# Gate and up of eight experts as three-part products with the high and low weights under 320 and 160 columns, their weights in 512 KB pieces over eleven half slots

## The chip, the cores and the metric

The kernel runs on 1 core of one Trainium2 chip. The metric is the device time of one execution in microseconds: 2761.57 us, the median of 3 runs.

## The reference, cut to what matters

A model of four layers over 512 tokens of width 1024: attention parts, feed-forward parts, a short convolution, and one layer of eight experts. The change touches the layer of experts. For each token two of eight experts are chosen, and each expert computes

```
h = silu(xb @ w_gate[e]) * (xb @ w_up[e])      # 1024 -> 1408
out = (h @ w_down[e]) * w                      # 1408 -> 1024
```

on the rows that chose it; the results are added to the tokens. Everything is float32. The weights of one expert are 3 x 1024 x 1408 numbers, 17.3 MB.

## The kernel before, in words

The program is one stream per engine, with semaphores between them and no scheduler: the order of each engine's work is the order of its Python loops. P is 128 and NE 8; KD = 8 tiles of 128 make the width of 1024, KE = 11 tiles of 128 make an expert's hidden width of 1408. Each expert has room for CAP = 160 rows: a main part of 128 and a tail of 32 (TAIL).

**Loads.** SP issues the weights in the order of a queue, `chunks`, which PE's code fills with `take_slot` (line 617): five ring slots of 1 MB, and each load first waits for the semaphore of the slot's last use. A gate and up chunk is one tile of 128 columns of each, so its rows in memory are 512 bytes long. Down chunks hold two tiles of 128 rows, 4 KB long each.

**Three-part products.** Most products of the kernel work on float32r numbers, in which a float32 is a high part, rounded by a copy, and a low part, the difference. `matmul3` issues high x high, high x low and low x high. In the other parts of the model POOL makes both parts of the weights (lines 2193 and 2195). In the experts' gate and up this was not done: `up_pairs` (line 989) calls `fmajor` (line 832), whose matmul at line 836 multiplies raw float32 weights by raw float32 tokens, 160 columns. The trace shows each such product as two weight loads and two matmuls.

**One expert.** PE runs 11 pairs of a gate and an up tile (line 836), then `down` (line 1234): the tails of six tiles at full precision (line 1252, four at a time beside each other, 32 weight columns each), the transposes that gather the next expert's rows (`gather`, line 1192), three-part products of the main rows (lines 1268 to 1270) for six tiles, the other five tails, and the last five tiles. ACT applies SiLU (line 1856), rounds h (line 1922) and the down weights (line 1917, three high buffers), copies the gathered tokens with their gain (line 1902), and stores the results (lines 1971 to 1981). DVE multiplies gate and up (line 2789) and makes the low parts of h (line 2982) and of the down weights (line 2994, in place of the raw ones).

**Beside it.** POOL prepares matrices for the S5 part of a later layer, from SBUF to SBUF, with one semaphore after most instructions (lines 2312 to 2475). Four times PE turns such matrices (`turn_s5`, line 1299), twice it multiplies them (`intra_runs`, line 1311), once it turns the last expert's slots. Before, these run beside the fourth tile of experts 1 to 5. In the last expert POOL fetches the other experts' results by row (line 2491) and DVE adds them, weighted, to the tokens (`add_results`, line 2966): eight additions of 1024 columns. `scatter_last` (line 1228) then puts the last expert's rows back by a product.

## Time and profile before

| | |
|---|---|
| Median of 3 runs | 2761.57 us (2757.92 to 2771.27) |
| Profiled execution, own time | 2766.07 us |
| Its span | 2764.3 us |
| PE busy | 2668.6 us (97%), 13787 matmuls |
| DVE busy | 1164.6 us (42%) |
| ACT busy | 766.2 us (28%) |
| POOL busy | 1609.5 us (58%) |
| Mean DMA rate over the span | 134 GB/s |

The times of single instructions come from the profiled execution. Matmuls are pipelined: the duration of one holds its way through the array, so the pace of a stream is read from the distance between starts, or from a count over a window. PEld is the weight load, which runs beside the matmul before it. The DMA share is the mean busy share of 16 DMA engines and can exceed 1 where packets wait in them.

### The profile page before, as it was taken

What the parts mean: (1) busy time and instruction counts of PE and PEld (TensorE: products, weight loads), DVE (VectorE), ACT (ScalarE), POOL (GpSimd) and SP (SyncE); (2) the same over time, 40 slices, a digit from 0 to 9 for tenths busy, and PEclk for the clock granted to TensorE, in tenths of its full rate; (3) what the DMA queues carried; (4) which work ended last, traced back from release to release, by engine and by line L of the source; (5) the groups of instructions that cost most, each with busy time, mean ns of one, the idle gap of its engine ahead of it and who ended that gap; (6) DMA issues with size and microseconds to landing.
All of it is one profiled execution on the core that took longest, in us unless ns stands there. A gap on an engine that the chain in (4) does not pass through costs nothing.

```text
span 2764.3 us, 36674 instructions
## 1 busy us (share of the span) xinstructions
PE 2668.6 (97%) x13787; PEld 2142.2 (77%) x13787; DVE 1164.6 (42%) x2147; ACT 766.2 (28%) x1812; POOL 1609.5 (58%) x1778
## 2 busy tenths in 40 slices
PE   7999899999999899999999899899999998999999
PEld 3536578888888799999989576788888876788887
DVE  1156623213256323222243626557165347365372
ACT  2256621001110223232322414522022226421120
POOL 2235477777777431524362353578788662688785
PEclk9999999999999999999999999999999999999999
DMA  6741033233433399989899522433332312533331
GB/s 190 177 107 31 1 89 95 84 107 103 140 117 91 109 265 280 276 267 299 251 282 286 190 62 76 119 92 99 99 100 69 100 46 102 139 92 95 100 100 42
DMA packets 449183, 371.06 MB, mean 134 GB/s; under 512 B 16926, under 2 KB 388327, under 8 KB 448362
## 3 DMA queue, kind: packets, MB, share of 16 engines
q1 hardware_dynamic: 429504, 321.62, 39.4%
q0 software_dynamic: 12240, 33.00, 4.0%
q10 hardware_dynamic: 7258, 14.03, 2.1%
q8 instruction: 113, 1.85, 0.3%
q14 instruction: 68, 0.56, 0.1%
HBM read 335.59 MB, written 32.41 MB: 133 GB/s over the span
## 4 chain that ended last, share of the span: by engine, by line
PE 90%; DVE 4%; issue 2%; ACT 2%; DMA 1%; POOL 1%; ACTq 0%; DVEq 0%; SPq 0%; POOLq 0%
PE bank L654 19%; PE bank L656 19%; PE bank L655 19%; PE bank L836 15%; PE bank L848 2%; PE bank L1268 1%; PE bank L1252 1%; PE bank L931 1%; PE bank L1269 1%; PE bank L1270 1%; PE bank L900 1%; PE bank L948 1%; PE bank L957 1%; PE bank L914 1%; PE bank L717 1%
## 5 line engine op out<-in xcount | busy, mean ns | idle before, releaser
L2195 POOL TENSOR_TENSOR unit_parts<-ring,unit_parts 128x512 fp32r<-128x512 f32 x580 | 807.8, 1393 | 48.4
L2193 POOL TENSOR_SCALAR unit_parts<-ring 128x512 fp32r<-128x512 f32 x580 | 427.3, 737 | 359.6 <-PE bank L656 323.5
L654 PE MATMUL bank<-x_hi,unit_parts 128*128 128x512 f32 x1408 | 553.2, 393 | 0.8 <-issue 0.8
L656 PE MATMUL bank<-x_hi,unit_parts 128*128 128x512 f32 x1408 | 548.4, 389 | 0.0
L655 PE MATMUL bank<-x_lo,unit_parts 128*128 128x512 f32 x1408 | 548.0, 389 | 0.0
L836 PE MATMUL bank<-arena,ring 128*128 128x160 f32 x2816 | 384.8, 299 | 0.8 <-ACT arena L1902 0.8
L836 PEld LDWEIGHTS bank<-arena,ring 128*128 128x128 f32 x2816 | 383.4, 190 | 1.8 <-ACT arena L1902 1.0
L654 PE MATMUL bank<-unit_parts,hid_parts 128*128 128x512 f32 x784 | 307.9, 393 | 2.4 <-DVE hid_parts L2724 1.8
L654 PEld LDWEIGHTS bank<-x_hi,unit_parts 128*128 128x128 f32 x1408 | 264.5, 188 | 57.8 <-issue 2.8
L656 PEld LDWEIGHTS bank<-x_hi,unit_parts 128*128 128x128 f32 x1408 | 264.3, 188 | 55.6
L655 PEld LDWEIGHTS bank<-x_lo,unit_parts 128*128 128x128 f32 x1408 | 264.5, 188 | 54.3 <-issue 1.0
L655 PE MATMUL bank<-unit_parts,hid_parts 128*128 128x512 f32 x784 | 305.2, 389 | 0.0
L656 PE MATMUL bank<-unit_parts,hid_parts 128*128 128x512 f32 x776 | 302.3, 390 | 0.0
L2154 ACT ACTIVATE arena<-arena,vec 128x512 f32<-128x512 f32 x88 | 71.9, 817 | 464.4 <-DVE arena L3222 464.4
L2735 DVE TENSOR_TENSOR x<-bank,x 128x512 f32<-128x512 f32 x80 | 55.2, 691 | 331.7 <-PE bank L656 331.7
L2789 DVE TENSOR_TENSOR arena<-bank,arena 128x160 f32<-128x160 f32 x88 | 28.6, 324 | 359.7 <-PE bank L836 352.2
L654 PEld LDWEIGHTS bank<-unit_parts,hid_parts 128*128 128x128 f32 x784 | 147.2, 188 | 33.6 <-issue 3.9
L655 PEld LDWEIGHTS bank<-unit_parts,hid_parts 128*128 128x128 f32 x784 | 147.3, 188 | 30.4 <-issue 0.5
L656 PEld LDWEIGHTS bank<-unit_parts,hid_parts 128*128 128x128 f32 x776 | 145.7, 188 | 30.7
L2994 DVE TENSOR_TENSOR ring_lo<-ring,down_hi 128x1024 fp32r<-128x1024 f32 x88 | 111.5, 1300 | 51.5 <-ACT down_hi L1917 31.7
L3226 DVE SCALAR_TENSOR_TENSOR arena<-arena,vec 128x511 f32<-128x511 f32 x88 | 79.0, 898 | 77.9 <-ACT arena L2154 77.9
L1917 ACT ACTIVATE down_hi<-ring 128x1024 fp32r<-128x1024 f32 x88 | 92.7, 1060 | 66.9 <-PE bank L1270 52.5
(398 smaller groups left out, 3602.6 us busy)
## 6 DMA issues: line engine op xcount, KB each, us to landing
ring<-in_moe_w_gate SPq DMA_DIRECT2D x88, 512.0 KB, 6.6
ring<-in_moe_w_up SPq DMA_DIRECT2D x88, 512.0 KB, 7.4
ring<-in_w_up SPq DMA_DIRECT2D x88, 512.0 KB, 5.1
ring<-in_moe_w_down SPq DMA_DIRECT2D x40, 1024.0 KB, 5.7
ring<-in_w_down SPq DMA_DIRECT2D x16, 1024.0 KB, 5.0
ring<-in_od_w_in SPq DMA_DIRECT2D x24, 512.0 KB, 4.5
ring<-in_ffn_w_gate SPq DMA_DIRECT2D x22, 512.0 KB, 4.0
ring<-in_ffn_w_up SPq DMA_DIRECT2D x22, 512.0 KB, 5.3
```

Source lines behind the costliest of these rows:

```text
L654: pe.matmul(ps, a[0], b[0], start=start, stop=False)
L655: pe.matmul(ps, a[0], b[1], start=False, stop=False)
L656: return pe.matmul(ps, a[1], b[0], start=False, stop=stop)
L836: ins = pe.matmul(ps[rows_at:rows_at + m, 0:n], w[:, k * width + at:k * width + at + m], src[:, k, :], start=k == 0, stop=k == KD - 1)
L848: ins = pe.matmul(ps[:, :], weights(k), xnT[:, k, :], start=k == 0, stop=k == KD - 1)
L1917: act.activation(down_hi[:, n % DOWN_HI, :], raw, ACT.Copy).then_inc(S("down_rounded"), 1)
L2154: act.activation(acc[:, 2 * a + n % 2, :], unscaled[:, a, :], ACT.Identity, scale=vcol("conv_w_2", 132 * l + 88 + f), bias=vcol("conv_b_2" ...
L2193: pool.tensor_scalar(hi, raw, 1.0, 1.0, ALU.mult, ALU.mult).then_inc(S("units_rounded"), 1)
L2195: pool.tensor_tensor(lo, raw, hi.bitcast(F32), ALU.subtract).then_inc(S("units_split"), 1)
L2735: drain(dve.tensor_tensor(xs, ps[:, :], xs, ALU.add), key)
L2994: dve.tensor_tensor(lo, raw, down_hi[:, n % DOWN_HI, :].bitcast(F32), ALU.subtract)\
L3226: link(dve.scalar_tensor_tensor(out=o[:, 1:T], in0=b[:, 0:T - 1], scalar=vcol("conv_w_2", 132 * l + 44 + f), in1=o[:, 1:T], op0=ALU.mult, ...
```

## The change

Gate and up become three-part products. The gathered tokens are kept as a high and a low part side by side, 320 columns (`xe`). For each weight tile PE issues two products into one PSUM bank: the high weights under all 320 columns, the low weights under the first 160. Columns 0 to 159 then hold high x high + low x high, and 160 to 319 hold high weights x low tokens. ACT copies the second half out (`copy_low`), DVE adds the first to it (`sum_parts`) and drains the bank. SiLU, the product of gate and up and both parts of h now work on blocks of two tiles (`BLOCKS` = 6, the last with one tile), in SBUF.

Weights come in 33 pieces of 512 KB per expert: 22 of gate and up, 11 of down. A gate or up piece is four tiles of rows by two tiles of columns, with rows of 1 KB, but for the last block's (eight by one, 512 bytes). ACT rounds every piece, four ahead of PE's, into one of six high buffers (three lie over the normed tokens, `xnT`); DVE makes every low part, three ahead, in place of the raw piece. The ring's slots are used as ten halves, and an eleventh half lies over `xnT`. So `xnT` is first saved to DRAM by a 2 MB transfer on ACT's queue (`xn_saved`); a rare branch for overfull experts loads it again. The first piece lands in that half, after the save.

The tails of the down weights are placed two tiles at a time from piece 18 on (`TAILS_AFTER`), the gathering of the next expert's rows after piece 25. The turns of S5 matrices move to the blocks in `TURNS_AT`, into PSUM banks that the next block uses. In the last expert the additions of results stand after DVE's last split. The first expert's tokens wait for both parts before PE starts. The tail of the last expert's results is split after its main rows instead of before. The core of the diff (declarations, the branch for overfull experts and what is removed are left out; the removed functions are told above):

```diff
+BLOCKS = (KE + 1) // 2
+UP_PIECES = 4 * (KE // 2) + 2
+PIECES = UP_PIECES + KE
+TAILS_AFTER = {UP_PIECES - 4 + k: tuple(range(k, min(k + 2, KE))) for k in range(0, KE, 2)}
+GATHER_AT = UP_PIECES + 3
+HALVES = 11
 DOWN_HI = 3
+HI_BUFS = DOWN_HI + 3
+ROUND_AHEAD, SPLIT_AHEAD = 4, 3
+TURNS_AT = {(1, 1): ("turn", 0), (1, 4): ("turn", 1), (2, 2): ("intra", 0), (3, 1): ("turn", 2),
+            (3, 4): ("turn", 3), (4, 2): ("intra", 1), (5, 1): ("slots", 0)}
+OVER_BANKS = 4
...
+        xn_dram = nc.dram_tensor("normed_turned", (P, KD * T), F32).ap()
...
+            half_at, slot_users = [0], {}
+            xn_kept = [None, (), (S("xn_saved"), 16), None]
+            def take_half(part):
+                i = half_at[0]
+                half_at[0] = (i + 1) % HALVES
+                if not pieces:
+                    slot_users.update(users[0])
+                slot, second = divmod(i - own_halves, 2)
+                earlier = users[0].get(SLOTS + i) or (slot_users.get(slot) if slot >= 0 else xn_kept)
+                entry = [SLOTS + i, (part,), None, earlier]
+                users[0][SLOTS + i] = entry
+                if slot >= 0:
+                    users[0][slot] = entry
+                chunks.append(entry)
+                of, at = (landed, slot) if slot >= 0 and second else (landed_half, i)
+                of[at] += 16
+                return i, (half_landed[i], of[at]), entry
...
+            def turned_by(e, at):
+                return (at + e) % BANKS
+            def piece_source(e, p):
+                if p >= UP_PIECES:
+                    k = p - UP_PIECES
+                    return 1, D, A["moe_w_down"][0, e][k * P:(k + 1) * P, :]
+                b, up = p // 4, p % 2
+                W = A["moe_w_up" if up else "moe_w_gate"][0, e]
+                if b == BLOCKS - 1:
+                    return KD, P, W[:, 2 * b * P:(2 * b + 1) * P]
+                k0 = 4 * (p % 4 // 2)
+                return 4, 2 * P, W[k0 * P:(k0 + 4) * P, 2 * b * P:(2 * b + 2) * P]
+            def take_pieces(last):
+                for n in range(len(pieces), last + 1):
+                    kn, w, src = piece_source(*divmod(n, PIECES))
+                    i, arrived, entry = take_half((0, kn, w, src))
+                    pieces.append(dict(raw=half_raw[i], lo=half_lo[i], hi=piece_hi[n % HI_BUFS], arrived=arrived,
+                                       used=None, entry=entry))
+            def used_by(n, done):
+                pieces[n]["used"] = pieces[n]["entry"][2] = done
+            def rows_used(ins):
+                used[0] += 1
+                ins.then_inc(S("rows_used"), 1)
+                return S("rows_used"), used[0]
+            def up_piece(n):
+                e, p = divmod(n, PIECES)
+                b, up = p // 4, p % 2
+                take_pieces(n)
+                kn, w, _ = piece_source(e, p)
+                jn, k0 = w // P, 0 if kn == KD else 4 * (p % 4 // 2)
+                last = k0 + kn == KD
+                if k0 == 0:
+                    for j in range(jn):
+                        claim(("up", f"moe{e}", 2 * b + j, up), at=turned_by(e, 4 * (b % 2) + jn * up + j))
+                piece = pieces[n]
+                pe.wait_ge(S("piece_split"), n + 1)
+                for j in range(jn):
+                    key = ("up", f"moe{e}", 2 * b + j, up)
+                    ps = bank(key)
+                    for k in range(k0, k0 + kn):
+                        cols = slice((k - k0) * w + j * P, (k - k0) * w + (j + 1) * P)
+                        if k == KD - 1:
+                            pe.matmul(ps[:, 0:CAP], piece["lo"][:, cols], xe[:, k, 0:CAP], start=False, stop=False)
+                            ins = pe.matmul(ps[:, 0:2 * CAP], piece["hi"][:, cols], xe[:, k, :], start=False, stop=True)
+                        else:
+                            pe.matmul(ps[:, 0:2 * CAP], piece["hi"][:, cols], xe[:, k, :], start=k == 0, stop=False)
+                            ins = pe.matmul(ps[:, 0:CAP], piece["lo"][:, cols], xe[:, k, 0:CAP], start=False, stop=False)
+                    if last:
+                        fill(ins, key)
+                used_by(n, filled_sem(key) if last else rows_used(ins))
...
+            def down_rows(n):
+                e, p = divmod(n, PIECES)
+                k = p - UP_PIECES
+                if k == 0:
+                    for m in range(2):
+                        claim(("y", e, m), at=turned_by(e, 7 + m))
+                piece = pieces[n]
+                pe.wait_ge(S("piece_split"), n + 1)
+                pe.wait_ge(S("hidE_split"), BLOCKS * e + k // 2 + 1)
+                for m in range(2):
+                    cols = slice(m * 512, (m + 1) * 512)
+                    ins = matmul3(bank(("y", e, m))[:, :], (hidE_hi[:, k, :], hidE_lo[:, k, :]),
+                                  (piece["hi"][:, cols], piece["lo"][:, cols]), k == 0, k == KE - 1)
                     if k == KE - 1:
+                        fill(ins, ("y", e, m))
+                used_by(n, filled_sem(("y", e, 1)) if k == KE - 1 else rows_used(ins))
+            def down_tail(n):
+                e, p = divmod(n, PIECES)
+                k = p - UP_PIECES
+                take_pieces(n)
+                if k == 0:
+                    claim(("y", e, 2), at=turned_by(e, 6))
+                tail, piece = bank(("y", e, 2)), pieces[n]
+                pe.wait_ge(*piece["arrived"])
+                pe.wait_ge(S("hid_made"), KF + BLOCKS * e + k // 2 + 1)
+                for q in range(4):
+                    ins = pe.matmul(tail[32 * q:32 * q + 32, 0:256], hidE[:, k, P:CAP],
+                                    piece["raw"][:, 256 * q:256 * q + 256], start=k == 0, stop=k == KE - 1)
+                if k == KE - 1:
+                    fill(ins, ("y", e, 2))
+                else:
+                    ins.then_inc(S("raw_read"), 1)
...
+            for n in range(NE * PIECES):
+                e, p = divmod(n, PIECES)
+                if p == 0:
+                    for k0 in range(0, KD, PER_BANK):
+                        wait_drained(pe, ("xg", e, k0))
+                if p < UP_PIECES:
+                    up_piece(n)
+                    if p % 4 == 2 and (e, p // 4) in TURNS_AT:
+                        turn_runs(e, p // 4)
+                else:
+                    down_rows(n)
+                for k in TAILS_AFTER.get(p, ()):
+                    down_tail(PIECES * e + UP_PIECES + k)
+                if p == GATHER_AT and e + 1 < NE:
+                    gather(e + 1)
...
+            for half in range(2):
+                wait_drained(act, ("nt", "od_ffn", NT - 1, half))
+            act.dma_start(xn_dram.rearrange("p (k t) -> p k t", k=KD), xnT[:, :, :]).then_inc(S("xn_saved"), 16)
...
+            def round_piece(n):
+                act.wait_ge(*pieces[n]["arrived"])
+                if n >= HI_BUFS:
+                    act.wait_ge(*pieces[n - HI_BUFS]["used"])
+                act.activation(pieces[n]["hi"], pieces[n]["raw"], ACT.Copy).then_inc(S("piece_rounded"), 1)
+            def copy_low(e, b, up):
+                n = BLOCKS * e + b
+                if n >= 2:
+                    act.wait_ge(S("hid_made"), KF + n - 1)
+                for j in tiles_of(b):
+                    ps = wait_filled(act, ("up", f"moe{e}", j, up))
+                    act.activation((ups if up else gates)[n % 2][:, j % 2, :], ps[:, CAP:2 * CAP], ACT.Copy)\
+                       .then_inc(S("lows_copied"), 1)
+            def gate(e, b):
+                n = BLOCKS * e + b
+                wait_drained(act, ("up", f"moe{e}", tiles_of(b)[-1], 0))
+                g = gates[n % 2][:, 0:len(tiles_of(b)), :]
+                act.activation(g, g, ACT.Silu).then_inc(S("silu_done"), 1)
+            def round_hid(e, b):
+                n = BLOCKS * e + b
+                act.wait_ge(S("hid_made"), KF + n + 1)
+                cols = slice(tiles_of(b)[0], tiles_of(b)[-1] + 1)
+                act.activation(hidE_hi[:, cols, :], hidE[:, cols, 0:P], ACT.Copy).then_inc(S("hidE_rounded"), 1)
...
+            for n in range(DOWN_HI):
+                round_piece(n)
+            act.wait_ge(S("xn_saved"), 16)
+            for n in range(DOWN_HI, ROUND_AHEAD):
+                round_piece(n)
             gather(0)
+            for n in range(NE * PIECES):
+                e, p = divmod(n, PIECES)
+                if n + ROUND_AHEAD < NE * PIECES:
+                    round_piece(n + ROUND_AHEAD)
+                if e and p == 2:
+                    store_y(e - 1)
+                if p % 4 == 0 and (e, p // 4 - 1) in TURNS_AT:
+                    turn_runs(e, p // 4 - 1)
+                for b in range(BLOCKS):
+                    gate_at, up_at = (4 * b + 2, 4 * b + 3) if b < BLOCKS - 1 else (UP_PIECES - 2, UP_PIECES - 1)
+                    if p == gate_at + 2:
+                        copy_low(e, b, 0)
+                    if p == up_at + 2:
+                        copy_low(e, b, 1)
+                    if p == up_at + 4:
+                        gate(e, b)
+                    if p == up_at + 6:
+                        round_hid(e, b)
+                if e == 0 and p == 20:
+                    load_first_rows()
+                if p == GATHER_AT + 2 and e + 1 < NE:
                     gather(e + 1)
+            store_y(NE - 1)
...
+            def split_piece(n):
+                e, p = divmod(n, PIECES)
+                dve.wait_ge(S("piece_rounded"), n + 1)
+                if p == PIECES - 1:
+                    wait_filled(dve, ("y", e, 2))
+                elif p >= UP_PIECES:
+                    dve.wait_ge(S("raw_read"), (KE - 1) * e + p - UP_PIECES + 1)
+                dve.tensor_tensor(pieces[n]["lo"], pieces[n]["raw"], pieces[n]["hi"].bitcast(F32), ALU.subtract)\
+                   .then_inc(S("piece_split"), 1)
+            def split_tokens(e):
+                for k0 in range(0, KD, PER_BANK):
+                    ps = wait_filled(dve, ("xg", e, k0))
+                    rows_n[0] += 1
+                    dve.wait_ge(S("rows_rounded"), rows_n[0])
+                    for k in range(k0, min(KD, k0 + PER_BANK)):
+                        ins = dve.scalar_tensor_tensor(out=xe[:, k, CAP:2 * CAP], in0=ps[:, (k - k0) * CAP:(k - k0 + 1) * CAP],
+                                                       scalar=vcol("od_ffn_norm", k), in1=xe[:, k, 0:CAP].bitcast(F32),
+                                                       op0=ALU.mult, op1=ALU.subtract)
+                    drain(ins, ("xg", e, k0))
...
+            def sum_parts(e, b, up):
+                to = (ups if up else gates)[(BLOCKS * e + b) % 2]
+                for j in tiles_of(b):
+                    key = ("up", f"moe{e}", j, up)
+                    lows_n[0] += 1
+                    dve.wait_ge(S("lows_copied"), lows_n[0])
+                    drain(dve.tensor_tensor(to[:, j % 2, :], bank(key)[:, 0:CAP], to[:, j % 2, :], ALU.add), key)
+            lows_n = [0]
+            def multiply(e, b):
+                n = BLOCKS * e + b
+                jn = len(tiles_of(b))
+                wait_drained(dve, ("up", f"moe{e}", tiles_of(b)[-1], 1))
+                dve.wait_ge(S("silu_done"), KF + n + 1)
+                dve.tensor_tensor(hidE[:, 2 * b:2 * b + jn, :], ups[n % 2][:, 0:jn, :], gates[n % 2][:, 0:jn, :], ALU.mult)\
+                   .then_inc(S("hid_made"), 1)
+            def split_hid(e, b):
+                n = BLOCKS * e + b
+                cols = slice(tiles_of(b)[0], tiles_of(b)[-1] + 1)
+                dve.wait_ge(S("hidE_rounded"), n + 1)
+                dve.tensor_tensor(hidE_lo[:, cols, :], hidE[:, cols, 0:P], hidE_hi[:, cols, :].bitcast(F32), ALU.subtract)\
                    .then_inc(S("hidE_split"), 1)
+            for n in range(SPLIT_AHEAD):
+                split_piece(n)
+            split_tokens(0)
+            for n in range(NE * PIECES):
+                e, p = divmod(n, PIECES)
+                if n + SPLIT_AHEAD < NE * PIECES:
+                    split_piece(n + SPLIT_AHEAD)
+                for b in range(BLOCKS):
+                    gate, up = (4 * b + 2, 4 * b + 3) if b < BLOCKS - 1 else (UP_PIECES - 2, UP_PIECES - 1)
+                    if p == gate + 3:
+                        sum_parts(e, b, 0)
+                    if p == up + 3:
+                        sum_parts(e, b, 1)
+                    if p == up + 5:
+                        multiply(e, b)
+                    if p == up + 7:
+                        split_hid(e, b)
+                if e in (2, 4) and 14 <= p < 22:
+                    add_skip(e // 2 - 1, p - 14)
+                if e == 0 and p == 20:
+                    mark_slots(NE - 1)
+                if p == GATHER_AT + 3 and e + 1 < NE:
+                    split_tokens(e + 1)
+                if e == NE - 1 and p >= PIECES - 4:
+                    for i in (2 * (p - PIECES + 4), 2 * (p - PIECES + 4) + 1):
                         add_results(i, got[:, i, :], w12[:, i:i + 1])
```

## Rows read from the trace of the kernel before

**Rows 1.** The page: the span, and the engines' shares of the chain that ended last

```profile
span 2764.3 us, 36674 instructions
...
PE 90%; DVE 4%; issue 2%; ACT 2%; DMA 1%; POOL 1%; ACTq 0%; DVEq 0%; SPq 0%; POOLq 0%
...
```

**Rows 2.** The chain in order of time; start us, us, what

```profile
...
965.48 48.08 PE bank L836 x352
...
1036.50 17.39 PE bank L836 x128
1053.89 1.75 PE bank L1299 x16
1055.64 30.43 PE bank L836 x224
1086.07 2.73 PE bank L1252 x48
1088.79 1.63 PE bank L1199 x16
...
1109.00 17.39 PE bank L836 x128
...
```

**Rows 3.** Windows: us, busy us (count) of PE, PEld, DVE, ACT, POOL, clock, DMA share, GB/s

```profile
965.00:1545.00 580.00, 571.61 (x4266) 519.42 (x4270) 177.28 (x287) 175.74 (x400) 212.87 (x353) 1.00 0.94 277
600.00:700.00 100.00, 100.00 (x443) 82.80 (x442) 32.54 (x38) 10.98 (x20) 76.01 (x74) 1.00 0.32 96
1037.00:1085.00 48.00, 48.00 (x359) 48.00 (x358) 9.02 (x19) 10.36 (x29) 7.58 (x7) 1.00 1.04 307
1448.00:1456.00 8.00, 8.00 (x61) 8.00 (x60) 1.05 (x4) 3.16 (x7) 0.00 (x0) 1.00 1.03 410
1161.00:1182.00 21.00, 20.92 (x136) 15.19 (x129) 12.93 (x10) 11.68 (x19) 20.18 (x29) 1.00 0.92 246
```

**Rows 4.** Timeline at the end of the stage; start us, us, engine, line

```profile
...
1515.54 2.60 DVE L2966 SCALAR_TENSOR_TENSOR x<-arena,small,x 128x1024 f32<-128x1024 f32 x2
...
1554.59 0.40 PE L1270 MATMUL bank<-down_hi,expert_lo 128*128 128x512 f32 x1
...
1555.82 0.47 PE L1228 MATMUL bank<-last_rows,last_slots 128*128 128x512 f32 x1 [0.83 <-issue]
...
```

**Rows 5.** Timeline in the first feed-forward part: a weight load and a matmul

```profile
...
700.00 0.39 PE L655 MATMUL bank<-unit_parts,hid_parts 128*128 128x512 f32 x1
700.00 0.19 PEld L656 LDWEIGHTS bank<-unit_parts,hid_parts 128*128 128x128 f32 x1
...
```

**Rows 6.** Timeline: PE's products of few columns

```profile
...
213.35 1.48 PE L948 MATMUL bank<-hid_parts,x_hi 128*128 128x32 f32 x12 [0.73 <-issue]
...
131.85 14.40 PE L1068 MATMUL bank<-arena,ring 128*128 128x62 f32 x128
...
```

**Rows 7.** DVE's and ACT's lines, 1037 to 1530: ns min/median/max, first and last start

```profile
L2994 DVE TENSOR_TENSOR ring_lo<-ring,down_hi x66: 1210/1224/3406, 1087.1 to 1477.2; 128x1024 fp32r<-128x1024 f32 x66
L2982 DVE TENSOR_TENSOR expert_lo<-arena,expert_hi x76: 274/281/4357, 1045.5 to 1529.4; 128x128 fp32r<-128x128 f32 x76
L2789 DVE TENSOR_TENSOR arena<-bank,arena x77: 309/325/326, 1041.0 to 1529.2; 128x160 f32<-128x160 f32 x77
L1917 ACT ACTIVATE down_hi<-ring x69: 1039/1061/1084, 1075.8 to 1528.2; 128x1024 fp32r<-128x1024 f32 x69
```

**Rows 8.** The logits' copy in the timeline, and a load in the page's DMA issues

```profile
...
946.70 0.60 ACT L1894 ACTIVATE arena<-bank 128x512 f32<-128x512 f32 x1 [5.45 <-PE bank L1165]
...
ring<-in_moe_w_down SPq DMA_DIRECT2D x8, 512.0 KB, 3.5
```

**Rows 9.** Timeline: DVE beside POOL

```profile
...
1060.33 4.36 DVE L2982 TENSOR_TENSOR expert_lo<-arena,expert_hi 128x128 fp32r<-128x128 f32 x1
...
1060.49 4.05 POOL L2432 TENSOR_TENSOR arena<-arena,cst 128x512 f32<-128x512 f32 x4
...
1386.21 10.13 DVE L2994 TENSOR_TENSOR ring_lo<-ring,down_hi 128x1024 fp32r<-128x1024 f32 x5
...
```

287 lines of the change are left out of this document (105 added, 182 removed).

## The prediction, made blind

> **What bounds the kernel now.** I read the page first: the span, and the chain that ended last, which is 90% PE [rows 1]. So the kernel is bound by TensorE's stream, and a stage gets shorter only where that stream does, or where PE waits. Next the chain in order of time, for the experts' stage [rows 2]. It starts at 965.48 and repeats per expert: from 1036.50 to 1109.00 is 72.50 us. Of that 17.39 + 30.43 = 47.82 us are the 352 records of the gate and up products. There are 88 weight tiles each for gate and up, 176 products, and each full-precision product stands as two records of 137 ns (48.08/352), so 273 ns a product. 1.75 us is a turn of S5 matrices. The rest, 22.93 us, is the down stage and the gathering of the next expert's rows. Its work is 66 down products, 88 tail records (48 in 2.73 us, so 5.0 us) and 1.63 us of transposes. In steady state a product of 512 columns costs 100/443 = 226 ns [rows 3], so the down products are 14.9 to 15.1 us, and the work is 21.7 us. About 1.2 us of each expert is waiting. From 965.48 to the scatter's first matmul at 1555.82 [rows 4] are 590.3 us. 8 x 47.82 + 8 x 21.7 - 1.6 (the last expert gathers nothing) is 554.6 us. The turns are 15.6 us: four of 1.75 us, and some 8.6 us for the intra runs and the slots, an estimate. So about 20.1 us are waits, spread over the down stages, the sixth and the last expert. DVE, ACT and POOL are busy for 177, 176 and 213 us of 580 in the stage [rows 3]: mostly idle, so they cost nothing so far.
>
> **The change, part by part.**
>
> *Products.* 176 full-precision products of 160 columns per expert become 176 pairs: the high weights under 320 columns, the low under 160. What does a pair cost? The wide one: 320/512 of 226 ns is 141 ns. Its floor is the row in which the same 320 column passes cost 137 ns [rows 2]. The narrow one has 160 columns, 71 ns by proportion. But a load of 128 weight columns starts only when the matmul before it has started: PEld L656 starts with PE L655 at 700.00 [rows 5]. Where matmuls are short, that load sets the pace. 12 products of 32 columns take 1.48 us, (1.48 - 0.25)/11 = 112 ns each, and 128 records of 62 columns take 14.40 us, (14.40 - 0.28)/127 = 111 ns each [rows 6] (0.25 and 0.28 us are the tail of the last one alone). Both are far above what their columns need. Between 71 and 141 ns I take 111.5 ns for the narrow product. The pair is 252.5 ns, and 176 of them are 44.4 us against 47.82: 3.4 us per expert, 27.4 us in all.
>
> The Trainium skill, TensorE: Matmul & The Clock Gate, section LDWEIGHTS (loading the stationary operand), gives a weight load as columns / 1.2, which is 107 ns for 128. That rule speaks against the narrow products, and the trace agrees with 111 to 112 ns. The section Back-to-back issue gap has about 81 ns for 128 columns and 131 for 512. By it the narrow product would be some 85 ns and the sum 37 us lower; the trace's 226 ns for 512 and 111 ns for 62 speak against it.
>
> *DVE.* It now splits all 33 pieces of an expert instead of 11 [rows 7]: 33 x 1.22 = 40.3 us. It adds 22 sums of 160 columns out of PSUM at 0.325 = 7.2 and 8 token differences at 0.325 = 2.6. The products and low halves of h now go by pairs of tiles. Interpolated between 0.28 us (128 columns) and 1.22 us (1024), 320 columns are 0.48 and 256 are 0.41 us, with single tiles last: 2.7 + 2.3 us. Sum 55.1 us, against PE's 44.4 + 21.7 = 66.1. It is hidden, with 11 us to spare per expert, and its lead is three pieces.
>
> *ACT.* 33 roundings at 1.06 = 35.0, 22 copies at about 0.3 (DVE's 0.325 for the same size) = 6.6, SiLU and rounding of h about 5, tokens, results and DMA issues about 8: 55 us of 66. Hidden. ACT's wait for a used high buffer lies six pieces back, for arrival four ahead, so what stands behind either wait (copies, SiLU) is not late.
>
> *Loads.* 277 GB/s x 580 us is 160.7 MB, 20.1 MB per expert [rows 3]. In 66.1 us that is 304 GB/s. While gate and up load in rows of 512 bytes, the DMA engines are full at 307 GB/s; while down loads in rows of 4 KB, they are full at 410 [rows 3]. Most gate and up rows become 1 KB, and the down share is a third, so I take 340 to 350 GB/s: hidden, but at nine tenths.
>
> *Waits removed.* Down weights are split a piece at a time, three ahead, with their tails placed earlier. The 1.2 us per expert and the losses of the sixth and last expert should go: -20.1 us.
>
> *Start.* x's normed rows are saved first (2 MB on ACT's queue, issued after the logits' copy at 946.70 [rows 8]), and the first piece lands in their place. All later pieces stand behind that wait on SP's queue. At 300 GB/s plus about 2 us the save ends near 956. A 512 KB piece lands in 3.5 us [rows 8], three are rounded and split by 965, and the tokens' low halves by 967.5. Against 965.48 that is +2 us, with 0 and 10 as bounds.
>
> *End.* In the last expert the eight additions of results move from beside the up stage to behind DVE's last split, and cost 2.60/2 = 1.30 us each [rows 4], 10.4 us. That split waits for the last tail, after piece 28. PE then has four pieces of 1.37 us, 5.5 us. DVE adds until 11.8 us, then splits y and the tail (3 us), so the scatter starts 15 us after that tail and not 5.5 + 1.0 (1555.82 less 1554.59 and its 0.23): +8.5 us, and I add 3 us for a clock that falls after such a pause, an estimate. Between 0 and 15.
>
> *DVE against POOL.* POOL's matrices of S5 need SBUF too. Beside short POOL instructions DVE's splits took 12.93/10 = 1.29 us instead of 1.22 (window 1161 to 1182 [rows 3]); beside POOL instructions of 512 columns five splits took 10.13 us, 2.03 each; one difference of 0.28 us took 4.36 beside four POOL instructions of 1 us in a row [rows 9]. Short ones cost 44 x 0.07 = 3 us per expert, within DVE's spare. The long ones, some 40 us in all, hold DVE up for about as long; its lead covers roughly two thirds. On the path: +12 us, bounds 0 and 110 (rival B). The turns claim banks that the next block of products needs, +2 us.
>
> Sum: -27.4 - 20.1 + 2 + 11.5 + 12 + 2 = -20 us. The profiled execution took 2766.1 us (span 2764.3), so 2746. That execution was 4.5 us above the median of the three runs (2761.57), so the median after should be 2741.6, 0.7% less.
>
> **The rivals.**
>
> A, *the narrow product costs its columns*: 71 ns. The pair is 212 ns, 176 are 37.2 us, 57 us less in all. DVE and ACT at 55 us then stand against 58.9, and I give back 17: 2702 us. For it: the rows at 111 ns are none of 160 columns. Against: two different lines agree on them. 12%.
>
> B, *the SBUF port between DVE and POOL becomes the bound*, slower. Place: POOL's work between turn 1 and the tables, while DVE splits all the time. Were each of POOL's 213 us a DVE stop, the stage would need 8 x 55.1 + 213 = 654 us against PE's 543, +110. It decides from half of that overlap on. POOL is slowed too, and PE waits for its matrices at the third turn and the intra runs. I take half of the excess: +50, so 2792 us. For it: the 2.03 and 4.36 us above. Against: 1.29 us in a window where POOL was busy for 20.18 of 21 us. 24%.
>
> The Trainium skill, SBUF — State Buffer, section Who interferes with whom, says that a DVE instruction with two SBUF inputs and a GpSimd instruction that reads SBUF block each other for a whole instruction. By it rival B would be the likelier; the 2.03 us agree with it, the 1.29 us show how little short instructions cost.
>
> C, *the pair is no cheaper*: if weights of the new form cost their load in full between products, 137 ns each, the up stage stays at 47.8 us and the change gives 2769. 8%.
>
> D, *the loads bind*: if 1 KB rows go no faster than 307 GB/s, 20.1 MB take 65.5 us, as much as PE, and every jitter shows, some 3 us per expert: 2766. 12%.
>
> **How the numbers follow.** My forecast has 44%. A measurement here can tell about 0.5% (13.8 us) from no change. Faster than 2747.8: 0.37 of my case, A's 0.12, a little of D: 0.50. Within 0.5%: 0.07 of mine, most of C and D: 0.22. Slower: B but for a little, parts of C and D: 0.28. The range runs from A's 2702, with 4 us below it, to B's 2792, with 4 above.
>
> **What would show it.** In the changed profile: pairs of 320 and 160 columns at 250 to 256 ns, so an up stage of 44 to 45 us; if 212, A; if 273, C. A period of 66 to 68 us where POOL is idle. DVE busy for some 450 us in the stage, its splits at 1.2 to 1.3 us; if many take 2 us and PE waits on the splits, B. PE waiting on loads, with the DMA share at 1, is D. At the end, a pause of about 9 us before the scatter.

## The result, and the profile after

The changed kernel is slower: 2776.47 us (median of 10 runs, 2770.68 to 2778.65) against 2761.7 us in runs beside it, a ratio of 1.0044 with an interval of 1.003 to 1.0058. The ratio is estimated from all the runs and is not the quotient of the two medians, which would be 1.0053. I had forecast 2741.6.

The page of the kernel after, against [rows 1]: the path is still PE's, and DVE's share of it has grown.

```profile
span 2771.6 us, 37515 instructions
...
PE 2662.2 (96%) x13787; PEld 2124.0 (77%) x13787; DVE 1454.9 (52%) x2483; ACT 968.4 (35%) x2084; POOL 1689.1 (61%) x1778
...
PE 86%; DVE 6%; issue 3%; ACT 2%; DMA 2%; POOL 1%; ACTq 0%; SPq 0%; DVEq 0%; POOLq 0%
```

Windows of the stage and of its end (columns as in [rows 3]):

```profile
965.00:1545.00 580.00, 569.84 (x4322) 504.23 (x4323) 463.05 (x613) 376.27 (x668) 292.94 (x350) 1.00 0.89 286
1330.00:1360.00 30.00, 25.59 (x215) 24.47 (x215) 29.84 (x26) 17.23 (x28) 24.62 (x21) 1.00 0.88 288
1550.00:1560.00 10.00, 5.23 (x10) 2.50 (x10) 5.82 (x10) 0.34 (x1) 7.91 (x9) 0.55 0.00 0
1560.00:1570.00 10.00, 10.00 (x19) 4.31 (x18) 3.20 (x5) 1.66 (x3) 3.23 (x4) 0.50 0.34 108
```

DVE is busy for 463 us of the 580, where it was 177. From 1330 to 1360 it has no idle time and PE loses 4.4 us. After 1550 TensorE's clock is at half: the scatter runs at 0.50.

Who PE waited for in the stage (the view of waits, PE alone; us in total, times, longest):

```profile
PE bank L1286 <- DVE last_rows L3212: 9.1, 1, 9.1
PE bank L1346 <- DVE ring_lo L3134: 4.9, 5, 1.5
PE bank L1267 <- DVE arena L3156: 2.5, 1, 2.5
PE bank L710 <- DVE ring_lo L3134: 1.1, 2, 0.8
```

And the end in the timeline, PE's rows and then DVE's, where before the scatter began 1.2 us after the last down product [rows 4]:

```profile
1545.26 0.40 PE L712 MATMUL bank<-x_hi,expert_lo 128*128 128x512 f32 x1
1554.77 0.76 PE L1286 MATMUL bank<-last_rows,last_slots 128*128 128x512 f32 x1 [9.11 <-DVE last_rows L3212]
...
1541.14 10.52 DVE L3113 SCALAR_TENSOR_TENSOR x<-arena,small,x 128x1024 f32<-128x1024 f32 x8
1551.70 1.29 DVE L3208 TENSOR_TENSOR last_rows<-bank,last_rows 128x512 fp32r<-128x512 f32 x2
1552.91 1.71 DVE L3212 TENSOR_TENSOR last_rows<-bank,last_rows 32x256 fp32r<-32x256 f32 x4
```

**Where the time went.** I cut both executions at the same places and added up PE's steps from the start of one instruction to the start of the next; a step above 0.36 us counts as 0.25 us of work and the rest as a wait. From the router's first product to the product with which the next stage sets in again (1594.4 before, 1603.1 after):

| part | before | after | difference | forecast |
|---|---|---|---|---|
| router's product to first gate product | 22.1 | 24.4 | +2.3 | +2 |
| gate and up products, 8 experts | 383.5 | 368.6 | -14.9 | -27.4 |
| down products, tails, gathers | 178.7 | 185.5 | +6.8 | 0 |
| turns | 15.7 | 15.7 | 0.0 | +2 (banks) |
| waits in the stage but for the last | 11.6 | 10.4 | -1.2 | -20.1 + 12 |
| pause before the scatter | 1.0 | 9.3 | +8.3 | +8.5 |
| scatter | 10.2 | 17.8 | +7.6 | +3 (the clock) |
| scatter to the next stage's start | 28.4 | 30.5 | +2.1 | |
| sum | 651.1 | 662.1 | +11.0 | -20 |

+11.0 us agrees with the ratio (0.44% of 2762 is 12.2 us; the medians lie 14.8 us apart). The profiled executions differ by only 7.3 us in span, because the one of after reached the router's product 2.4 us earlier and the one of before had another 1.4 us more behind this stretch; neither lies in what was changed. So the stage up to its last down product gained 9.3 us (-14.9 + 6.8 - 1.2), and its two ends lost 20.3: 2.3 at the start, and 18.0 from the pause on.

### The profile page after: what moved, and what is told of

Read it like the earlier page. It is cut to its first block, busy times and chain, and to the rows that moved or that the text cites. A ratio compares the mean times of both kernels' runs of the same rounds, so it can differ in the third digit from the quotient of the medians.

```text
span 2771.6 us, 37515 instructions
## 1 busy us (share of the span) xinstructions
PE 2662.2 (96%) x13787; PEld 2124.0 (77%) x13787; DVE 1454.9 (52%) x2483; ACT 968.4 (35%) x2084; POOL 1689.1 (61%) x1778
## 3 DMA queue, kind: packets, MB, share of 16 engines
q8 instruction: 113, 1.85, 0.3%
## 4 chain that ended last, share of the span: by engine, by line
PE 86%; DVE 6%; issue 3%; ACT 2%; DMA 2%; POOL 1%; ACTq 0%; SPq 0%; DVEq 0%; POOLq 0%
PE bank L710 20%; PE bank L712 20%; PE bank L711 20%; PE bank L1346 7%; PE bank L1347 3%; DVE ring_lo L3134 2%; PE bank L892 2%; PE bank L904 1%; PE bank L1381 1%; PE bank L987 1%; PE bank L1344 1%; PE bank L956 1%; PE bank L1004 1%; PE bank L970 1%; PE bank L1013 1%
## 5 line engine op out<-in xcount | busy, mean ns | idle before, releaser
L1347 PE MATMUL bank<-expert_x,ring_lo 128*128 128x160 f32 x1120 | 265.5, 237 | 0.0
L1347 PEld LDWEIGHTS bank<-expert_x,ring_lo 128*128 128x128 f32 x1120 | 214.0, 191 | 0.0
L3134 DVE TENSOR_TENSOR ring_lo<-ring,down_hi 128x1024 fp32r<-128x1024 f32 x120 | 168.3, 1418 | 37.2 <-PE bank L1381 21.0
L3134 DVE TENSOR_TENSOR ring_lo<-ring,x_hi 128x1024 fp32r<-128x1024 f32 x120 | 160.6, 1354 | 45.0 <-ACT x_hi L2035 28.8
L1346 PE MATMUL bank<-expert_x,down_hi 128*128 128x320 f32 x616 | 166.5, 344 | 5.6 <-DVE ring_lo L3134 3.9
L711 PEld LDWEIGHTS bank<-unit_parts,hid_parts 128*128 128x128 f32 x784 | 147.3, 188 | 30.5 <-issue 0.5
L1346 PE MATMUL bank<-expert_x,x_hi 128*128 128x320 f32 x616 | 165.8, 344 | 1.0 <-DVE ring_lo L3134 1.0
```

What stands on the lines that cost most here:

```text
L711: pe.matmul(ps, a[0], b[1], start=False, stop=False)
L1346: pe.matmul(ps[:, 0:2 * CAP], piece["hi"][:, cols], xe[:, k, :], start=k == 0, stop=False)
L1347: ins = pe.matmul(ps[:, 0:CAP], piece["lo"][:, cols], xe[:, k, 0:CAP], start=False, stop=False)
L3134: dve.tensor_tensor(pieces[n]["lo"], pieces[n]["raw"], pieces[n]["hi"].bitcast(F32), ALU.subtract)\
```

## The experiments

All times are against the kernel before in the same session. "Stretch" is the sum of the table above, in the one execution that was profiled (651.1 before, 662.1 after).

**1. The additions earlier.** DVE's eight additions of results leave the end.

```diff
-                if e == NE - 1 and p >= PIECES - 4:
-                    for i in (2 * (p - PIECES + 4), 2 * (p - PIECES + 4) + 1):
-                        add_results(i, got[:, i, :], w12[:, i:i + 1])
+                if e == NE - 1 and 19 <= p < 27:
+                    add_results(p - 19, got[:, p - 19, :], w12[:, p - 19:p - 18])
```

> The changed kernel with one edit: the eight additions of results stand one behind each of DVE's pieces 19 to 26 of the last expert, not two behind each of its last four. Theory (late end): the 9.26 us from the last down product (1545.3) to the scatter (1554.8) and the 8.6 us that the scatter and what follows then take longer at half clock both come from these additions. DVE idles some 14 us between 1508 and 1541, so they fit there: the pause falls to about 1 us, the clock stays at 1.0, the time falls by 15 to 18 us against the changed kernel, to 2758 to 2762, ratio to the kernel before 0.998 to 1.000. Rival (DVE is full): the additions delay the splits, PE stops in the last expert's down stage for as long as it gained, and the ratio stays at 1.003 to 1.004.

Measured: 2771.1 us, ratio 1.0018 (1.0007 to 1.0029). By the ratios this is 7 us less than the changed kernel, of the 15 to 18 expected; in the stretch of the profiled execution (2773.06 us as a whole, over the median) it is 1.9 us. The scatter ran at half clock there as before. Windows of this run:

```profile
1520.00:1530.00 10.00, 10.00 (x94) 8.15 (x86) 9.75 (x12) 6.40 (x13) 0.31 (x1) 1.00 1.02 349
1530.00:1540.00 10.00, 10.00 (x71) 6.62 (x64) 9.86 (x13) 4.32 (x6) 0.00 (x0) 1.00 0.74 224
```

Eight additions of 1.3 us in 22 us fill DVE, so that it is late with the last splits: PE stops for 1.3 us at 1547.0. The 3.3 us at 1549.8 have another cause: ACT and DVE split the y rows and only then the tail rows, the order that the change brought in. Both theories were partly right. The two stops, together 4.7 us, stand before a scatter that takes 17.8 us.

**2 and 3. The pause filled.** Forty products whose result is overwritten, ahead of the scatter's waits. In the first try they took the scatter's next bank, which was still the tail's, and so stood behind the pause; in the second they took a free one.

```diff
+                next_bank[False] = 0        (second try only)
+                ps = claim(first)
+                for _ in range(40):
+                    pe.matmul(ps[:, :], slotT[:, 0, 0:P], slotT[:, 0, :], start=True, stop=True)
                 wait_drained(pe, ("y", NE - 1, 2))
```

> The changed kernel with 40 more products of 512 columns (1 bank, overwritten later) between the last down product and the scatter, about 9.1 us of work in a pause of 9.26 us. Theory (the clock falls because PE stands still): the scatter starts where it did, within 1 us, but at clock 1.0, its matmuls take 0.33 us apart and not 0.56 to 0.60, and the stretch from the scatter's first matmul to the next stage's first product falls from 24.0 to about 15 us: 8 to 9 us less in all, ratio 1.001. Rival (the clock falls there for what the stage asked before): the scatter still runs at 0.5, and the time is no lower, ratio 1.004.

> The changed kernel with the same 40 products of 512 columns as in the run before, now in a bank that is free, so that they stand in the pause and not behind it. Theory (the clock falls because PE stands still): they run at 0.23 us each from 1545 on, the scatter starts within 1 us of where it did and takes 10 us, not 18; 8 to 9 us less than the changed kernel, ratio 1.001. Rival (the clock falls for another reason): the scatter takes 18 us, ratio 1.004 or more.

Measured: 2780.55 us, ratio 1.0052 (1.0037 to 1.0068) for the first; 2767.45 us, 1.0005 (0.999 to 1.002) for the second. PE's timeline of the second:

```profile
1543.97 0.39 PE L712 MATMUL bank<-x_hi,expert_lo 128*128 128x512 f32 x1
1544.20 9.23 PE L1282 MATMUL bank<-last_slots 128*128 128x512 f32 x40
1553.39 0.50 PE L1291 MATMUL bank<-last_rows,last_slots 128*128 128x512 f32 x1
1553.73 0.40 PE L1292 MATMUL bank<-last_rows,last_slots 128*128 128x512 f32 x1
```

The scatter starts 9.4 us after the last down product, as it did, but takes 10.3 us. With useless work in the pause the kernel is some 10 us faster than the changed one by the ratios, 7.1 in the stretch: the clock fell because PE stood still. In the first try the forty took 12.2 us instead of 9.2, the scatter 10.1: the clock came back during them. They start 0.43 us apart up to about 1564.6, 5.5 us after the first of them, and 0.23 apart from then on.

**4. Tails in four places, not six.**

```diff
-TAILS_AFTER = {UP_PIECES - 4 + k: tuple(range(k, min(k + 2, KE))) for k in range(0, KE, 2)}
+TAILS_AFTER = {UP_PIECES - 3 + k: tuple(range(k, min(k + 3, KE))) for k in range(0, KE, 3)}
```

> The changed kernel with the tails' few-column matmuls in four places per expert (3, 3, 3, 2 tiles) and not in six (2 each). Theory (each place costs a restart): a switch from products to tails and back costs 0.33 + 0.31 us where a product's step is 0.23, and the first product after it 0.34 in place of 0.23, about 0.3 to 0.5 us a place; two places less in eight experts are 5 to 8 us less in the stage. Rival (lead): split of a down piece must wait for its tail, which now comes a piece later, so that PE waits on DVE's splits in the down stage, 0.5 us or more per expert, and the time stays or rises by up to 10 us.

Measured: 2792.48 us, ratio 1.0096 (1.0082 to 1.0111): the rival, and more of it than it said. In the seventh expert, where DVE is on time, tails, down and up products together took 67.04 us against 67.84, 0.4 us per place saved. Everywhere else the splits came late. Its waits:

```profile
PE bank L710 <- DVE ring_lo L3134: 9.0, 7, 2.9
PE bank L710 <- issue: 7.1, 4, 3.7
```

A down piece cannot be split before its tail has read the raw weights, since the low part overwrites them. So six places are the price of DVE's lead of three pieces; a longer lead was not tried.

**5. POOL without its tables.** The doubling loop is left out.

```diff
-                link(pool.memset(tab_cos[:, :, 0:1], 1.0))
-                link(pool.memset(tab_sin[:, :, 0:1], 0.0))
-                for k in range(RUNS.bit_length() - 1):
+                link(pool.memset(tab_cos, 1.0))
+                link(pool.memset(tab_sin, 0.0))
+                for k in range(0):
```

> The changed kernel without POOL's doubling loop for the S5 tables (the tables hold ones; their build is left out, 14 rounds of six operations, most of the 63 us that POOL is busy between 1330 and 1400). Theory (DVE is slowed beside POOL): the fifth expert's period falls from 75.9 us to 72 to 73 us, its three waits of PE on DVE (0.98, 0.95 and 2.55 us) are gone, and L3134 there takes 1.25 us, not 1.6; the whole gets 3 to 5 us shorter. Rival (the waits come from the order of DVE's own work, the skip additions and the turn's banks): the period stays within 1 us of 75.9.

Measured: 2772.85 us, ratio 1.0024 (1.0012 to 1.0036), about 5.5 us less than the changed kernel. The period from 1323.24 to 1394.15 is 70.9 us (75.9), the next 69.3 (71.05), the one before 75.3 (73.9): 5.3 us in the three. That is a net figure: without the tables POOL's next long operations come earlier, and one of them makes a stop of 1.3 us at 1313.7. What happens there in the changed kernel, POOL's row and then DVE's:

```profile
1335.55 12.26 POOL L2459 TENSOR_TENSOR arena<-arena 128x512 f32<-128x512 f32 x4
...
1334.37 7.88 DVE L3134 TENSOR_TENSOR ring_lo<-ring,down_hi 128x1024 fp32r<-128x1024 f32 x3
1342.17 7.85 DVE L3134 TENSOR_TENSOR ring_lo<-ring,x_hi 128x1024 fp32r<-128x1024 f32 x3
```

The six splits take 2.6 us each on average instead of 1.22. One by one they go with POOL's instruction beside them: 2.3 us beside those of 512 columns and 3.4 beside those of 1024 (POOL's merged row holds both). The rival, the order of DVE's own work, explains little of it.

**6. The tables spread.** The end as in experiment 8, and each of POOL's table operations of 512 and 1024 columns waits for a split.

```diff
+                def pace(k):
+                    if k == RUNS.bit_length() - 2:
+                        pool.wait_ge(S("piece_split"), PIECES * 5 + 27 * l + 2 + 5 * next(heavy) // 2)
...
+                    pace(k)
                     pool.tensor_tensor(ta, tab_sin[:, :, 0:n], wi, ALU.mult)
```

> As the first run of this call, and POOL's tables are spread: each of their operations of 512 columns waits for a DVE split, one per 2.5 pieces, over the sixth and seventh experts (1336 to 1460), where the changed kernel does them in two bursts of 22 us (1326 to 1348, 1378 to 1398). Theory (DVE has 14 us to spare per expert, and only a burst outruns its lead of three pieces): the waits of PE on DVE in these two experts fall from 6.1 us to under 1.5, their periods from 75.9 + 71.05 to 142 or 143 in all: 4 to 5 us less. Rival (each such operation costs DVE its own length wherever it stands, and DVE is the bound of these experts): the waits only move into the seventh expert, and the sum of the two periods stays within 1.5 us of 147.

Measured: 2760.16 us, ratio 0.9982 (0.9971 to 0.9993), no different from experiment 8 without it. The two periods are 75.35 + 71.46 = 146.8 us, against 77.43 + 70.31 = 147.7 there. The rival holds: the waits moved and kept their sum (2.96 us at 1370.8 and 1.54 us at 1445.2 took the places of the old ones).

**7. What a pair costs.** Other column counts in three experts.

```diff
+                wide, low = {1: (2 * CAP, 32), 2: (CAP, CAP), 3: (2 * CAP, 2 * CAP)}.get(e, (2 * CAP, CAP))
...
-                            ins = pe.matmul(ps[:, 0:CAP], piece["lo"][:, cols], xe[:, k, 0:CAP], start=False, stop=False)
+                            ins = pe.matmul(ps[:, 0:low], piece["lo"][:, cols], xe[:, k, 0:low], start=False, stop=False)
```

> The changed kernel with other column counts in three experts' pairs: in the second the narrow product has 32 columns, in the third both have 160, in the fourth both have 320 (the last three quarters of the low parts left out, or the low parts counted where they are not wanted; the first product of a group keeps its 320). Theory (the larger of the columns and a weight load, each product by itself): 141 + 112 = 253 to 257 ns for 320 and 32, 2 x 112 = 223 for 160 and 160, 2 x 141 = 282 for 320 and 320; against 257 for 320 and 160. Rival (columns alone): 155, 141 and 282. Rival (a fixed cost for each pair): 257 minus 56 = 200 for 320 and 32, 187 for 160 and 160, and 327 for 320 and 320.

PE's timeline in the second, third and fourth expert of this run, and in the seventh, which is as in the changed kernel:

```profile
1056.13 0.39 PE L1348 MATMUL bank<-expert_x,down_hi 128*128 128x320 f32 x1
1056.36 0.18 PE L1349 MATMUL bank<-expert_x,ring_lo 128*128 128x32 f32 x1
1056.39 0.39 PE L1348 MATMUL bank<-expert_x,down_hi 128*128 128x320 f32 x1
...
1134.15 0.28 PE L1349 MATMUL bank<-expert_x,x_hi 128*128 128x160 f32 x1
1134.26 0.28 PE L1348 MATMUL bank<-expert_x,x_hi 128*128 128x160 f32 x1
1134.37 0.27 PE L1349 MATMUL bank<-expert_x,x_hi 128*128 128x160 f32 x1
...
1200.92 0.30 PE L1349 MATMUL bank<-expert_x,ring_lo 128*128 128x320 f32 x1
1201.06 0.31 PE L1348 MATMUL bank<-expert_x,down_hi 128*128 128x320 f32 x1
1201.21 0.31 PE L1349 MATMUL bank<-expert_x,ring_lo 128*128 128x320 f32 x1
...
1420.45 0.35 PE L1348 MATMUL bank<-expert_x,x_hi 128*128 128x320 f32 x1
1420.63 0.23 PE L1349 MATMUL bank<-expert_x,ring_lo 128*128 128x160 f32 x1
1420.70 0.34 PE L1348 MATMUL bank<-expert_x,x_hi 128*128 128x320 f32 x1
```

Pairs take 258 ns (320 and 32; from 1055.61 to 1056.90 five of them), 222 ns (160 and 160), 290 ns (320 and 320) and 257 ns (320 and 160). Over each whole expert the medians are 258, 224, 293 and 259 ns. So a narrow product costs 111 ns whether it has 32 columns or 160, and a wide one 145 ns, and the two add up: 145 + 111 = 256. The theory's form is right, its 141 ns is 4 ns too low. Both rivals are out. This is one execution, and the paces are read inside it.

**8. The end spread.** Additions behind every second piece, tail rows split ahead of the y rows; first with POOL's gathers of results at every piece, then as in the changed kernel at every second one.

```diff
+                if e == NE - 1 and 11 <= p < 27 and p % 2:
+                    i = (p - 11) // 2
+                    add_results(i, got[:, i, :], w12[:, i:i + 1])
...
-                    pool.wait_ge(S("piece_split"), PIECES * (NE - 1) + 6 + 2 * i)
+                    pool.wait_ge(S("piece_split"), PIECES * (NE - 1) + 6 + i)      (first run only)
```

> The changed kernel with the end rearranged: the eight additions of results stand behind every second of DVE's pieces 11 to 25 of the last expert, POOL gathers their rows one per piece from piece 6 on, and ACT and DVE split the tail rows before the y rows. Theory (a stop of 3 us and more costs the clock as well): in the run with the additions from piece 19 on, DVE was busy 9.8 of 10 us from 1520 to 1540, PE stopped 1.3 and 3.3 us before the scatter, and the scatter ran at half clock all the same; from piece 11 on DVE has some 2 us idle in ten, so that the stops shrink to under 2 us, the scatter runs at 1.0 and its 18 us become 10: 2758 to 2762, ratio 0.998 to 1.000. Rival (DMA): the 2 MB of gathered rows come while the loads already take all of the DMA engines (1.04 to 1.07), the pieces of the last expert land late, and the up stage loses 3 to 6 us: ratio 1.002 or more.

> As the run with spread additions, but POOL gathers the rows of results at every second piece again, as the changed kernel does. Theory (the 4.15 us stop at 1513.5 in that run is a late load, pushed back by the quicker gathers): the stop is gone, the last expert takes 82 to 84 us from its gather to the scatter and not 87.7, the pause before the scatter stays at 1 us and the scatter at 1.0: 4 us less than that run, ratio to the kernel before 0.997 to 0.999. Rival (the additions themselves hold up DVE's splits): a stop of 3 us or more stays in the last expert's up stage, ratio 0.999 to 1.001.

Measured: 2764.18 us, ratio 0.9994 (0.998 to 1.0009), and 2759.47 us, ratio 0.998 (0.9968 to 0.9992). In both the pause is 1.0 us and the scatter takes 10.2 us. In the first run PE stopped for 4.15 us at 1513.5; from its chain:

```profile
1495.23 16.78 DMA ring<-in_moe_w_gate
1512.03 1.07 ACT x_hi L2035
1513.13 1.23 DVE ring_lo L3134
```

with these windows:

```profile
1500.00:1510.00 10.00, 10.00 (x80) 10.00 (x79) 6.76 (x11) 3.71 (x7) 4.54 (x7) 1.00 1.04 334
1510.00:1520.00 10.00, 5.94 (x47) 4.50 (x46) 6.91 (x11) 6.79 (x13) 0.30 (x1) 0.90 1.02 381
```

A load took 16.8 us to land, with the DMA engines full. With the old pace of the gathers the stop is gone, and the last expert takes 82.0 us from its gather to the scatter (87.7, and 90.3 in the changed kernel).

**9. The start and the slots.** With the end of the first run of 8: the first gather's banks, and the turn of the slots in the seventh expert.

```diff
-                    ps = claim(("xg", 0, k0), at=4 + k0 // PER_BANK)
+                    ps = claim(("xg", 0, k0), at=5 + k0 // PER_BANK)
-            (3, 4): ("turn", 3), (4, 2): ("intra", 1), (5, 1): ("slots", 0)}
+            (3, 4): ("turn", 3), (4, 2): ("intra", 1), (6, 1): ("slots", 0)}
```

> The end rearranged as in the run with spread additions, and two edits more: the first gather's products take the banks 5, 6 and 7 and not 4, 5 and 6 (bank 4 is still read by DVE for the places), and the turn of the slots stands in the seventh expert and not in the sixth. Theory: the gather starts 2.1 us earlier (idle before it 1.8 and not 3.9 us), and the wait of 2.5 us for a bank that DVE drains late beside POOL's tables goes; with the end 2754 to 2758, ratio 0.996 to 0.998. Rival: PE then waits in the sixth expert for DVE's next split instead, and the start is bound by the weights (ACT rounds the fourth piece at 960.0 before the tokens), so that nothing is gained beside the end.

Measured: 2767.84 us, ratio 1.0008 (0.9994 to 1.0022): nothing gained, the rival. The first gate product still comes 24.3 us after the router's (24.4): the gather starts 2.1 us earlier, but PE then stands for 4.3 us instead of 1.7, until DVE has made the tokens' low parts. The sixth expert's period fell to 72.85 us, the seventh's rose to 75.76; PE's waits in the two are 7.7 us (6.1 in the changed kernel). Taking PE's turn away from DVE's congested time only makes PE wait for DVE that much more.

**10. Loads first.** As the second run of 8, and the ring begins at half slot 1.

```diff
-            half_at, slot_users = [0], {}
+            half_at, slot_users = [1], {}
```

> As the run before in this call, and the first piece lands in the ring's half slot 1 and not in xnT, so that SP's loads no longer wait for the save of xn (issued at 943.0, landed at 949.8); the half in xnT comes eleventh. Theory (the first expert runs behind its loads): its stops (1.5 and 0.3 us) and the slow first pieces (57.97 us to its gather where a later expert takes 56.1) go, 2 to 3 us less. Rival (both share the DMA engines, and the gather of tokens, done at 963.7, sets the start anyway): within 1 us of the run before.

Measured: 2758.42 us, ratio 0.9978 (0.9964 to 0.9992). From its first product to its gather the first expert takes 55.9 us, in the run before 59.3 and in the changed kernel 58.0; the stretch is 644.2 us. The trace shows the 3 us; the two times cannot be told apart (their intervals overlap almost whole). Its ratio is the lowest of the study, 0.22% below the kernel before; experiment 6 and the second run of 8 are as good within their intervals.

| kernel | stretch, us | ratio |
|---|---|---|
| before | 651.1 | 1 |
| after | 662.1 | 1.0044 |
| additions earlier (1) | 660.2 | 1.0018 |
| pause filled too late (2) | 667.1 | 1.0052 |
| pause filled in time (3) | 655.0 | 1.0005 |
| tails by three (4) | 678.0 | 1.0096 |
| no tables (5) | 657.8 | 1.0024 |
| tables spread, end spread (6) | 647.8 | 0.9982 |
| end spread, quick gathers (8) | 651.2 | 0.9994 |
| end spread, old gathers (8) | 647.4 | 0.998 |
| start and slots (9) | 653.3 | 1.0008 |
| loads first (10) | 644.2 | 0.9978 |

## Why the prediction was wrong

I forecast 20 us less than the kernel before; it takes 11 to 15 us more. The step that failed is the one that took a remainder for waits; the terms of the products and of the clock were mis-sized. By my steps:

*Products: the mechanism was right, one term was mis-sized.* The narrow product costs 111 ns whatever its columns, as [rows 6] said; that this is its weight load was argued, not tested. Rivals A (71 ns) and C (137 ns) are out: the run of experiment 7 shows 111 ns at 32 and at 160 columns. For the wide one I took 320/512 of 226 ns, the 512-column pace of [rows 3] at 600 to 700. In the experts' stage itself a down product takes 234 ns before and 232 after from start to start (medians), and 320/512 of 233 is 145.6, which is what the wide product measured. A row beside the change would have been the better one to scale from. But it is not shown that this is the reason: a line through 145 ns at 320 columns and 226 at 512 leaves 10 ns a product besides its columns, an estimate, and would explain as much. 4.5 ns on 1408 pairs are 6.3 us. The other 6 us of the term's error are small steps, which I had counted nowhere: about 1 us each for the first pairs after a tail batch, for the switches to tails and for the swapped order at the end of each tile, and the rest for splits slightly late.

*Waits removed: this is the step that failed.* I took a remainder, 590.3 less my sum of work, 20.1 us, called it waits, and let the change remove all of it. In the trace of before only 12.6 us are stops of PE, 1.0 of it the pause before the scatter. What most of them waited for, in the view of waits of the stage before:

```profile
PE bank L1268 <- DVE ring_lo L2994: 5.0, 9, 1.7
PE bank L1252 <- DMA ring<-in_moe_w_down: 3.5, 1, 3.5
```

So DVE's splits already cost PE 5.0 us, where I had written that DVE cost nothing. Two of these stops, 1.85 and 1.83 us, belong to the splits beside POOL in [rows 9], and nothing in a change that splits three times as much would end that kind of wait. The rest of the remainder, 7.5 us, is in steps a little longer than the steady pace around them: a switch from products to tails costs 0.33 us, the way back 0.31, the product after it 0.34 instead of 0.23. The change does not remove these; it has six such places per expert where there were two, so the tails grew from 40.2 to 44.6 us and the down products from 126.9 to 129.9. And the stops it did remove came back in almost the same amount, 10.4 us against 11.6: some 7.5 us of them behind splits beside POOL's long operations, 1.5 behind a late load in the first expert. My +12 for DVE against POOL had room for these; the restarts had no term. A clean period shows it: before 72.50 - 1.75 = 70.75 us [rows 2]; after, in the seventh expert, 1464.66 - 1393.61 = 71.05. In the run without tables it is 69.3, which is 45.9 for the pairs, 16.3 for the down products, 5.6 for the tails and 1.6 for the gather, where I had 44.4 + 21.7. The changed kernel's seventh expert in the chain, with its stop for ACT's and DVE's late work from 1397.8 to 1399.4:

```profile
1393.61 1.48 PE bank L1257 x16
...
1396.69 1.04 PE bank L1381 x16
1397.80 1.57 issue
1399.37 1.21 DVE ring_lo L3134
...
1464.66 1.48 PE bank L1257 x16
```

*The start.* +2.3 us against +2. It does not come from the save: with the loads ahead of it (experiment 10) the first gate product comes no earlier (24.4). But the first expert then ran 2 us behind its loads, all queued behind the save of xn; I had put the queue into the start and not into the expert (experiment 10).

*The end: the pause was right, the clock was not.* Forecast 8.5, measured 8.3 us. For the clock I allowed 3 us; the scatter alone lost 7.6, since its 32 matmuls ran at half clock throughout, and 2.1 us more were lost up to the next stage's start. Experiments 3 and 8 show both sides: PE kept busy, or the pause cut to 1 us, and the scatter takes 10.2 us. Of the 2.1 us at least 1.0 is still there in these runs (29.4 to 30.7 us, 28.4 before); what causes it is open. The 3 us had been taken from no row. This term was 16 to 18 us, with an upper bound of mine at 15.

*DVE against POOL.* Forecast 12 us on the path. The tables cost 5.3 us net (experiment 5), in the sixth and seventh experts. Two stops more, 0.6 us at 1114.1 and 0.7 at 1261.1, each come behind two splits that take 5.4 us beside POOL operations of 1024 columns, and they are there without the tables too. Together that is some 7 us, within my bounds; rival B, 50 us, did not happen. DVE's busy time was foreseen (463 us measured, 450 forecast). Beside long POOL operations a split takes 2.0 to 5.0 us, as [rows 9] had with 2.03, but DVE's lead and idle time absorb the others. The Trainium skill, SBUF — State Buffer, section Who interferes with whom, has a VectorE instruction with two SBUF inputs and a GpSimd instruction that reads SBUF block each other for a whole instruction. Between 1334 and 1350 the trace agrees: six splits take 15.7 us. My +2 for banks stood for a wait that did occur, 2.5 us before the turn of the slots in the sixth expert; the table has it among the waits.

*Loads (rival D).* They did not bind in the stage as a whole (0.89 of the DMA engines, 286 GB/s), but at its two ends they did: in the first expert, by 2 us, and in the last as soon as the gathers of results came quicker (experiment 8).

So the sum went: -27.4 became -14.9 and +6.8, -20.1 + 12 + 2 became -1.2, and +13.5 at the two ends became +20.3: -20 became +11. The middle group misses by less than its first term does, since the 12 + 2 us allowed for new stops were more than the 10.4 that came; that was luck.

## What to carry to other kernels

A remainder between a measured period and a sum of steady paces is not waiting. Before a change is credited with it, look for the stops themselves in the trace, and price each switch between kinds of matmul; a change that cuts work into more batches adds switches. Scale a duration from a row of the same stage, and for another size look for a second row before taking it as proportional. And work that is moved off a busy stretch to the end of a stage costs twice: once as the pause, and again as a clock that stays low for all that follows it. Here that was 8 and another 8 to 10 us, and spreading the same eight operations over DVE's idle time, with the tail rows split first again, gave 8.3 and 7.6 us back.

## What the runs showed of the hardware

- A float32r product of 128 x 128 weights never took less than 111 ns, whether it had 32 or 160 columns. It took 145 ns with 320 and 232 to 234 with 512 in this stage, each product by itself: pairs of 257 to 259, 222 to 224 and 290 to 293 ns for the mixes of experiment 7.
- After the pause of 9.1 us the granted clock was 0.50, the lower of its two levels (1.2 GHz), for the whole scatter, though the view has PE busy throughout, from 1554.8 to 1572.6; its products start 0.56 to 0.59 us apart. In the first try of experiments 2 and 3 forty products at half clock start 0.43 us apart, and there the clock came back to 1.00 after 5.5 us. After stops of 1.3 and 3.3 us with a few products between them the scatter ran at 0.50 as well. After a pause of 1.0 us it stayed at 1.00.
- A DVE split (two SBUF inputs, 1024 columns) takes 1.22 us alone, 1.6 beside POOL operations of 256 columns, 2.0 to 2.3 beside those of 512 and 3.4 beside those of 1024 that read two tensors; once it took 5.0, as long as four POOL operations of 1.05 us in a row and itself.
